# Modulation products in four PSUM strips of 32 partitions, added by a selector product, with the first stage reordered

## The chip, the cores and the metric

The kernel is one program on one core of a Trainium2 chip. The metric is device time in microseconds (us) of one execution. TensorE is called PE (its weight loads PEld), VectorE DVE, ScalarE ACT, GpSimd POOL; SP issues most transfers. A matmul below is written by its stationary operand (partitions*columns) and its moving operand (partitions x columns). A matmul of f32 operands is two records of the trace (two weight loads and two streams of the moving operand); one of fp32r operands is one record.

## What is computed

Two transformer blocks over 512 tokens of width 1024. What the change touches is the modulation of the first block: two vectors of 1024 (`c` and `c_ctx`) go through silu and a 1024 x 6144 matrix, and the results shift, scale and gate what follows.

```python
mod_x = (jax.nn.silu(c) @ w_ada[l] + b_ada[l])[:, None, :]
mod_c = jax.nn.silu(c_ctx) @ w_ada[l] + b_ada[l]
sh1, sc1, g1, sh2, sc2, g2 = jnp.split(mod_x, N_MOD, axis=-1)
csh1, csc1, cg1, csh2, csc2, cg2 = jnp.split(mod_c, N_MOD, axis=-1)

p_x = modulate(rmsnorm(h, norm_mix_w[l]), sh1, sc1) @ w_in[l]
p_c = modulate(rmsnorm(hc, norm_mix_w[l]), csh1, csc1) @ w_in[l]
# gated linear attention over x with the context's state, pooling, output matmul,
# gate g1; then 32 experts (top 4) with sh2, sc2, g2; then the second block
```

`h` has 512 rows (x), `hc` 256 rows (context).

## The kernel before

**The modulation matrix** is worked in 12 chunks of 512 columns. Chunks 0 and 1 are the first shift, 2 and 3 the first scale, and so on in pairs. A chunk is four pieces of 512 KB (each two blocks k of 128 rows), fetched by SP into a ring of 9 slots (`W`, `fetch`, L437); piece i is issued when the work on piece i-9 is done. The weights of the input projection (`in_w_in`) follow the first four chunks in the same ring.

**A chunk** (`ada_pe`, L839) is eight f32 matmuls whose stationary operand has 2 columns (`cc`, the silu of the two vectors, in the tile SM) and whose moving operand is 128x512 of the ring. All eight add into 2 partitions of one PSUM bank. Then ACT copies the 2x512 result (`ada_act`, L868; `ada_row`), PE turns it in four small transposes into 128 x 8 (`adat`), and DVE adds the bias into MOD (`ada_dve`, `add_ada`, L884).

**The first stage** (`mod_pe`, `mod_act`, `mod_dve`) has 8 sum-of-squares matmuls for x (moving 128x512) and 8 for the context (128x256) against a matrix of ones. ACT squares into two buffers, so that square k waits for matmul k-2. Then come chunks 0, 2, 1, 3 in that order. DVE makes variance and reciprocal root for x and for the context (ACT takes the root), normalises 8 blocks of each in turn, and then, for each half h, adds the modulation of chunks h and h+2 (`gm`), and shifts and scales four blocks of each (`ntmp`, `hn_low`) into pairs of fp32r parts. The projection (`proj_pe`) starts with the parts of half 0 and with the first split unit of `in_w_in` (`conv_lo`, L465).

**The later chunks.** Chunks 4 to 9 are `slow` jobs: generators that PE, ACT and DVE advance between the steps of the gated linear attention (`gla_pe`, L1533), half a chunk at a time. Those that are left when the attention ends run one after the other (`finish_all`). Chunks 10 and 11 follow at the start of `out_pe` (L1922), ahead of the output matmul; their four small matmuls come inside it. `gla_pe` also has matmuls on 64 rows of the array at a time: the updates of the state (64*128 with 64x256) go to rows 0 to 63 and 64 to 127 in turn (`hh`, L1574), with the two taking turns in the program's order.

The order on each engine is the order in which this code issues; nothing reorders it.

Of the kernel before, what the change touches and what calls it, by code (L numbers as in the profile page):

```python
# [334 lines left out]
def build(nc, ins, out):  # L335
# [3 lines left out]
    def sb(name, shape, dt=F32):  # L339
        return nc.alloc_sbuf_tensor(name, shape, dt)  # L340
# [3 lines left out]
    COLS = sb("COLS", [128, 160])  # L344
    MOD = sb("MOD", [128, 96])
    SM = sb("SM", [128, 256])
    BPT = sb("BPT", [128, 1536])

    base = (nc.sbuf_base + 31) // 32 * 32
# [30 lines left out]
    def pe(*key):  # L380
        return s_pe, at_pe[key]
# [36 lines left out]
    def bank_of(name):  # L418
        return PB[banks[name]] if name in banks else PB[0]
# [59 lines left out]
    def raw_tile(w):  # L479
        return place(w.base, w.kt * w.n).rearrange("p (a b) -> p a b", b=w.n)  # L480
# [303 lines left out]
    def load_dve(v):  # L784
        for k in range(8):
            v.wait_ge(*pe("xt", k))
            v.copy(hk(k), bank_of(("xt", k))[:, :])
            v.free(("xt", k))
        for k in range(8):
            v.wait_ge(*pe("ct", k))  # L790
            v.copy(HC[:, k, :], bank_of(("ct", k))[:, 0:256])
            v.free(("ct", k))
        v.wait_ge(*pe("cols"))
        v.copy(COLS[:, 0:n0 + 48], bank_of("cols")[:, 0:n0 + 48])
        v.free("cols")

    cc = SM[:, 0:16].rearrange("p (k s) -> p k s", s=2)
    HXh, HXl, HCh, HCl = r(10496, 4096, 512), r(14592, 4096, 512), r(18688, 2048, 256), r(20736, 2048, 256)  # L800
    sq1 = [a(8448, 512), a(8960, 512)]
    rx, rc = a(9472, 512), a(9984, 256)
# [9 lines left out]
    def sumsq_act(q, tag, src, nk, T, sq):  # L812
        for k in range(nk):
            if k >= 2:
                q.wait_ge(*pe("sumsq", tag, k - 2))
            q.act(sq[k % 2][:, 0:T], src(k), ACT.Square, ("square", tag, k))
# [22 lines left out]
    def ada_pe(p, c):  # L839

        key = ("ada", c)
        b = p.bank(key)
        p.inuse.append(b)
        w = None
        for k in range(8):
            if k % 2 == 0:
                w = W.raws[RAW_ADA[c] + k // 2]
                land(p, w)
            if k == 0:
                p.wait_ge(*act("silu c"))  # L850
                p.claim(key)
            p.mm(PB[b][0:2, :], cc[:, k, :], raw_tile(w)[:, k % 2, :], k == 0, k == 7, count=k % 2 == 1)
            if k % 2 == 1:
                p.note(w.done)
            if k == 3:
                yield
        p.note(("ada", c))
        p.inuse.remove(b)
        yield
        b = p.bank(("adat", c))  # L860
        p.wait_ge(*act("ada", c))
        p.claim(("adat", c))
        mr = ada_row(c)
        for j in range(4):
            p.tp(PB[b][:, 2 * j:2 * j + 2], mr[:, j * 128:(j + 1) * 128], ("adat", c) if j == 3 else None)
        yield

    def ada_act(q, c):  # L868
        yield
        q.wait_ge(*pe("ada", c))  # L870
        if c > 4:
            q.wait_ge(*pe("adat", c - 1))
        q.copy(ada_row(c), bank_of(("ada", c))[0:2, :], ("ada", c))
        q.free(("ada", c))
        yield
        yield
# [15 lines left out]
    RAW_ADA = [4 * FIRST.index(c) if c < 4 else 25 + 4 * (c - 4) for c in range(12)]  # L892

    def ada_row(c):
        return ar[0:2, c * 512:c * 512 + 512] if c < 4 else ar[0:2, 22272:22784]

    def mod_act(q):
        q.limit = U_IN
        q.wait_ge(*dve("all", "cols"))
        q.act(cc[:, :, 0], C("c", 0, 8), ACT.Silu)  # L900
        q.act(cc[:, :, 1], C("cctx", 0, 8), ACT.Silu, "silu c")
        sumsq_act(q, "x", hk, 8, 512, sq1)
        root2_act(q, "x", rx)
        sumsq_act(q, "ctx", lambda k: HC[:, k, :], 8, 256, sq1)
        root2_act(q, "ctx", rc)
        for h in range(2):
            for c in (h, h + 2):
                for _ in ada_act(q, c):
                    pass
            q.wait_ge(*dve("gm", h))  # L910
            for k in range(4 * h, 4 * h + 4):
                for s in range(2):
                    q.act((HXh, HCh)[s][:, k, :], normed_in(s, k), ACT.Identity, ("hn high", s, k), bias=M(0, k, s), scale=gm[:, k, s:s + 1])
            for u in (2 * h, 2 * h + 1):
                conv_hi(q, W, u)
# [3 lines left out]
        return XN[:, k, :] if s == 0 else HC[:, k, :]  # L919

    def mod_pe(p):
        sumsq_pe(p, "x", 8, 512, sq1)
        sumsq_pe(p, "ctx", 8, 256, sq1)
        turn = []
        for c in FIRST:
            part = ada_pe(p, c)
            next(part)
            next(part)
            for x in turn:
                for _ in x:  # L930
                    pass
            turn = [part]
        for _ in turn[0]:
            pass

    def mod_dve(v):
        v.limit = U_IN
        root1_dve(v, "x", 8, 512, rx, 1.0 / 1024)
        root3_dve(v, "x", rx)
        root1_dve(v, "ctx", 8, 256, rc, 1.0 / 1024)  # L940
        root3_dve(v, "ctx", rc)
        for k in range(8):
            v.stt(XN[:, k, :], hk(k), C("nmix", k), rx, ALU.mult, ALU.mult)
            v.stt(HC[:, k, :], HC[:, k, :], C("nmix", k), rc, ALU.mult, ALU.mult)
        for h in range(2):
            for c in (h, h + 2):
                for _ in ada_dve(v, c):
                    pass
            v.ts(gm[:, 4 * h:4 * h + 4, :], mcol[:, 8 + 4 * h:12 + 4 * h, :], 1.0, None, ALU.add, None, ("gm", h))
            ahead = None  # L950
            for k in range(4 * h, 4 * h + 4):
                for s in range(2):
                    v.ts(ntmp[s][k % 2], normed_in(s, k), gm[:, k, s:s + 1], M(0, k, s), ALU.mult, ALU.add)
                    if ahead:
                        hn_low(v, *ahead)
                    ahead = (s, k)
            hn_low(v, *ahead)
            for u in (2 * h, 2 * h + 1):
                conv_lo(v, W, u)
# [917 lines left out]
    def last_ada_act(q):  # L1877
        yield
        q.wait_ge(*pe("adat", 10))
        q.copy(ada_row(11), bank_of(("ada", 11))[0:2, :], ("ada", 11))  # L1880
        q.free(("ada", 11))
        yield
        for _ in range(2):
            yield
# [7 lines left out]
    def out_act(q):  # L1892
        q.limit = None
        for u in range(NUNIT):
            conv_hi(q, W, U_IN + u)
            split_act(q, "mix", mixp, lambda k: MX[:, k, :], range(2 * u, 2 * u + 2))
        q.wait_ge(*pe("ada", 10))
        q.copy(ada_row(10), bank_of(("ada", 10))[0:2, :], ("ada", 10))
        q.free(("ada", 10))
        q.slow += [last_ada_act(q), shift_act(q)]  # L1900
        tile = lambda c, m: q.jobs.append(tile_act(q, c * 4 + m))
        dense(q, conv_hi, W, [512], 8, tile)
        by_tiles(q, 1, tile)
        q.u += 4
# [2076 lines left out]
```

## Time and profile before

| | us |
|---|---|
| median of 3 runs | 3268.64 (3266.44 to 3270.3) |
| span of the profiled execution | 3265.2 |
| PE busy in it | 3061.1 (94%) |
| DVE busy | 2139.1 (66%) |
| ACT busy | 1639.6 (50%) |
| share of PE in the chain that ended last | 82% |
| HBM read | 608.10 MB |

Times of the trace are counted from the start of its span. The first stage lies before 76.7 us, the projection up to 198.6, the attention up to 355, the output matmul from 374.8; the experts and the second block, which the change doesn't touch, fill the rest. A record of a matmul includes some 0.16 us of its way through the array, so that ten records in a row take less than ten times the mean; the distance between starts is what a matmul costs in a row of them. In `windows`, PEclk is the granted clock as a share of 2.4 GHz.

### The profile page before, as it was taken

How to read it: one execution, taken by the hardware profiler on the slowest of the kernel's cores; microseconds unless marked ns; L12 is line 12 of the kernel's file. 1: busy time of each engine (PE TensorE's matmuls, PEld its weight loads, DVE VectorE, ACT ScalarE, POOL GpSimd, SP SyncE). 2: the span in 40 equal slices, each digit the busy share in tenths (PEclk: the TensorE clock that was granted, in tenths of full speed). 3: DMA queues.
4: the chain of work that ended last, by engine and by line, in shares of the span. 5: the costliest groups of instructions: out<-in, count | busy, mean ns of one | idle time of the engine just before them, and what ended most of it. 6: DMA issues, size and time to landing. Idle time of an engine off the chain costs nothing.

```text
span 3265.2 us, 36970 instructions
## 1 busy us (share of the span) xinstructions
PE 3061.1 (94%) x13794; PEld 2398.3 (73%) x13794; DVE 2139.1 (66%) x2425; ACT 1639.6 (50%) x1933; POOL 261.3 (8%) x234
## 2 busy tenths in 40 slices
PE   6989989999999999999979977999998987999998
PEld 2865467777777777777767756888886765888887
DVE  4555449999999999999966444443446557443445
ACT  3332338878887788778753213332235237332334
POOL 1053720000000000000010000000000000000000
PEclk9998969999999999999988978999999997999999
DMA  6244749999999999999963202323232220223210
GB/s 214 70 132 155 234 157 375 363 378 373 377 364 372 379 376 372 363 377 377 363 205 134 84 29 88 96 91 103 91 108 74 84 59 1 84 91 103 91 65 26
DMA packets 225085, 643.10 MB, mean 197 GB/s; under 512 B 20054, under 2 KB 38516, under 8 KB 224036
## 3 DMA queue, kind: packets, MB, share of 16 engines
q1 hardware_dynamic: 207984, 577.70, 48.8%
q0 software_dynamic: 12816, 51.39, 5.7%
q10 hardware_dynamic: 4100, 11.59, 0.9%
q8 instruction: 110, 1.80, 0.2%
q14 instruction: 75, 0.61, 0.1%
HBM read 608.10 MB, written 32.51 MB: 196 GB/s over the span
## 4 chain that ended last, share of the span: by engine, by line
PE 82%; DVE 11%; ACT 3%; issue 2%; DMA 1%; DVEq 0%; ACTq 0%; SPq 0%; POOLq 0%
PE ps L272 80%; PE ps L288 3%; DVE arena L192 2%; DVE arena L203 2%; DVE arena L199 2%; ACT wunits L463 1%; DVE ring_r L471 1%; ACT arena L237 1%; DVE arena_r L203 1%; DVE arena L215 1%; DVE arena L211 1%; DMA arena<-in_ctx 1%; DVE arena_r L471 1%; DVE H L192 0%; DMA sum_scratch<-arena 0%
## 5 line engine op out<-in xcount | busy, mean ns | idle before, releaser
L471 DVE TENSOR_TENSOR ring_r<-ring,wunits 128x1024 fp32r<-128x1024 f32 x795 | 949.5, 1219 | 659.8 <-ACT wunits L463 636.2
L463 ACT ACTIVATE wunits<-ring 128x1024 fp32r<-128x1024 f32 x795 | 834.6, 1054 | 809.3 <-PE ps L272 797.3
L272 PE MATMUL ps<-arena_r,wunits 128*128 128x512 f32 (+1 forms) x3552 | 1111.9, 395 | 15.5 <-DVE arena_r L192 6.9
L272 PE MATMUL ps<-wunits,arena_r 128*128 128x512 f32 x3520 | 991.3, 399 | 7.0 <-DVE arena_r L192 7.0
L272 PEld LDWEIGHTS ps<-arena_r,wunits 128*128 128x128 f32 x3552 | 671.5, 190 | 165.1 <-issue 16.6
L272 PEld LDWEIGHTS ps<-wunits,arena_r 128*128 128x128 f32 x3520 | 658.5, 189 | 152.4 <-DVE arena_r L192 8.9
L272 PE MATMUL ps<-arena_r,ring_r 128*128 128x512 f32 (+1 forms) x1776 | 695.1, 391 | 0.0
L272 PE MATMUL ps<-ring_r,arena_r 128*128 128x512 f32 x1280 | 410.3, 391 | 0.0
L272 PEld LDWEIGHTS ps<-arena_r,ring_r 128*128 128x128 f32 x1776 | 337.5, 190 | 70.5
L471 DVE TENSOR_TENSOR arena_r<-arena,wunits 128x1024 fp32r<-128x1024 f32 x240 | 284.9, 1221 | 16.6 <-ACT wunits L463 9.4
L463 ACT ACTIVATE wunits<-arena 128x1024 fp32r<-128x1024 f32 x240 | 254.3, 1061 | 65.6 <-PE ps L272 63.5
L272 PEld LDWEIGHTS ps<-ring_r,arena_r 128*128 128x128 f32 x1280 | 241.1, 188 | 53.2 <-issue 2.2
L272 PE MATMUL ps<-arena 128*128 128x128 f32 (+11 forms) x1074 | 194.0, 368 | 42.6 <-DVE arena L207 15.2
L237 ACT ACTIVATE arena<-ps 128x512 f32<-128x512 f32 (+6 forms) x190 | 121.4, 639 | 197.0 <-PE ps L272 143.6
L272 PEld LDWEIGHTS ps<-arena 64*128 64x128 f32 (+5 forms) x1074 | 135.7, 203 | 101.9 <-issue 42.7
L288 PE MATMUL ps<-KC,arena 128*128 128x128 f32 (+3 forms) x854 | 126.4, 290 | 73.7 <-DVE arena L203 37.9
L288 PEld LDWEIGHTS ps<-KC,arena 128*128 128x128 f32 (+3 forms) x854 | 102.1, 151 | 105.7 <-DVE arena L203 54.7
L272 PE MATMUL ps<-arena_r 128*128 128x512 f32 (+3 forms) x520 | 160.0, 392 | 0.9 <-DVE arena_r L197 0.9
L237 ACT ACTIVATE arena<-arena 128x512 f32<-128x512 f32 (+5 forms) x140 | 73.7, 527 | 135.5 <-DVE arena L192 84.0
L2360 POOL DMA_INDIRECT sum_scratch<-arena x33 | 52.4, 1587 | 1037.3 <-ACT arena L237 1037.3
L192 POOL TENSOR_TENSOR ring<-ring 128x512 f32<-128x512 f32 (+5 forms) x90 | 105.5, 1173 | 193.5 <-DVE ring L192 140.4
L192 DVE TENSOR_TENSOR arena<-ps,arena 128x512 f32<-128x512 f32 (+1 forms) x115 | 78.7, 684 | 61.7 <-PE ps L272 51.2
(171 smaller groups left out, 1928.5 us busy)
## 6 DMA issues: line engine op xcount, KB each, us to landing
ring<-in_w_gu SPq DMA_DIRECT2D x382, 512.0 KB, 8.5
ring<-in_w_down SPq DMA_DIRECT2D x170, 512.0 KB, 6.1
arena<-in_w_gu SPq DMA_DIRECT2D x146, 512.0 KB, 8.2
arena<-in_w_down SPq DMA_DIRECT2D x94, 512.0 KB, 6.4
ring<-in_w_ada SPq DMA_DIRECT2D x48, 512.0 KB, 4.7
ring<-in_ffn_w_gate SPq DMA_DIRECT2D x44, 512.0 KB, 3.5
ring<-in_ffn_w_up SPq DMA_DIRECT2D x44, 512.0 KB, 3.5
ring<-in_ffn_w_down SPq DMA_DIRECT2D x40, 512.0 KB, 3.6
```

Of the source, the lines that this page charges most:

```text
L192: self.inc(self.e.tensor_tensor(o, x, y, op), key)
L199: self.inc(self.e.tensor_scalar(o, x, s1, s2, op0, op1), key)
L203: self.inc(self.e.scalar_tensor_tensor(out=o, in0=x, scalar=s, in1=y, op0=op0, op1=op1), key)
L211: self.inc(self.e.reciprocal(o, x), key)
L215: self.inc(self.e.tensor_reduce(o, x, AX.X, op), key)
L237: self.inc(self.e.activation(o, x, f, **kw), key)
L272: ins = self.e.matmul(o, l_, r_, start=start, stop=stop, skip_group_check=True)
L288: ins = self.e.transpose(o, x, self.ident[0:k, 0:k])
L463: q.inc(q.e.activation(h, raw, ACT.Copy), (st.tag, "hi", i))
L471: q.inc(q.e.tensor_tensor(lo, raw, h.bitcast(F32), ALU.subtract), (st.tag, "lo", i))
L2360: g.e.indirect_dma_start(out=sum_d, out_offset=bass.IndirectOffsetOnAxis(ap=idx, axis=0), in_=YB[i], in_offset=None, compute_op=ALU.add).t ...
```

## The change

- The silu values move from SM to a tile of their own, CW (48 columns, filled with zeros once). The stationary operand of product k is now the 32 columns from 2k on: its first two are the silu values of block k, the rest are those of later blocks or zeros.
- Product k writes PSUM partitions 32(k mod 4) to 32(k mod 4)+31. Blocks k and k+4 add up in one strip, so a bank holds four partial sums, with the wanted rows at partitions 0, 1, 32, 33, 64, 65, 96 and 97.
- ACT copies 128x512 in the place of 2x512. The four transposes become four ordinary f32 matmuls: stationary 128*128 of the copied rows, moving the 128x2 selector `strips`, which has a one where the partition is 0 or 1 within its strip; they turn and add the strips at once. DVE makes `strips` in the load stage, with a fill and a reduction, ahead of its copy of COLS.
- The first stage is in another order: products of chunks 0 and 2, sum of squares of x, small matmuls of chunks 0 and 2, products of chunks 1 and 3, sum of squares of the context, small matmuls of chunks 1 and 3. ACT and DVE follow that order. DVE now normalises all of x ahead of the variance of the context.
- Order and number of the products in the later stages stay as they are.

```diff
+    CW = sb("CW", [128, 48])
...
+        v.fill(CW[:, :], 0.0)
+        v.wait_ge(*loaded("kc"))
+        v.reduce(strips, ident.rearrange("p (j c) -> p c j", c=32)[:, 0:2, :], ALU.add)
         v.wait_ge(*pe("cols"))
         v.copy(COLS[:, 0:n0 + 48], bank_of("cols")[:, 0:n0 + 48])
...
-            p.mm(PB[b][0:2, :], cc[:, k, :], raw_tile(w)[:, k % 2, :], k == 0, k == 7, count=k % 2 == 1)
+            strip = slice(32 * (k % 4), 32 * (k % 4) + 32)
+            p.mm(PB[b][strip, :], CW[:, 2 * k:2 * k + 32], raw_tile(w)[:, k % 2, :], k < 4, k >= 4,
+                 count=k % 2 == 1)
...
-            p.tp(PB[b][:, 2 * j:2 * j + 2], mr[:, j * 128:(j + 1) * 128], ("adat", c) if j == 3 else None)
+            p.mm(PB[b][:, 2 * j:2 * j + 2], mr[:, j * 128:(j + 1) * 128], strips, j == 0, j == 3,
+                 ("adat", c) if j == 3 else None)
...
-        q.copy(ada_row(c), bank_of(("ada", c))[0:2, :], ("ada", c))
+        q.copy(ada_row(c), bank_of(("ada", c))[:, :], ("ada", c))
...
         sumsq_act(q, "x", hk, 8, 512, sq1)
+        for c in (0, 2):
+            for _ in ada_act(q, c):
+                pass
         root2_act(q, "x", rx)
         sumsq_act(q, "ctx", lambda k: HC[:, k, :], 8, 256, sq1)
+        for c in (1, 3):
+            for _ in ada_act(q, c):
+                pass
         root2_act(q, "ctx", rc)
...
+        for cs, tag, T in (((0, 2), "x", 512), ((1, 3), "ctx", 256)):
+            products = [ada_pe(p, c) for c in cs]
+            for x in products:
+                next(x)
+                next(x)
+            sumsq_pe(p, tag, 8, T, sq1)
+            for x in products:
                 for _ in x:
                     pass
```

PE at the start of the first stage, before (-) and now (+). `ring,SM` and `ring,CW` are products of chunks, `arena,KC` the sums of squares, `KC,arena` 128x2 the transposes and `SM,arena` 128x2 the selector products; the first number of a shape is the number of partitions written.

```order
+L272 MATMUL ps<-ring,CW 32x512 x16
 L272 MATMUL ps<-arena,KC 128x512 x8
+L272 MATMUL ps<-SM,arena 128x2 x8
+L272 MATMUL ps<-ring,CW 32x512 x16
 L272 MATMUL ps<-arena,KC 128x256 x8
-L272 MATMUL ps<-ring,SM 2x512 x16
-L288 MATMUL ps<-KC,arena 128x2 x4
-L272 MATMUL ps<-ring,SM 2x512 x8
-L288 MATMUL ps<-KC,arena 128x2 x4
-L272 MATMUL ps<-ring,SM 2x512 x8
-L288 MATMUL ps<-KC,arena 128x2 x8
+L272 MATMUL ps<-SM,arena 128x2 x8
```

The 32 products of the first four chunks stand 16 ahead of the sum of squares of x and 16 ahead of that of the context, where all stood behind both.

DVE in the load stage and the first stage, before (-) and now (+); COLS holds the transposed vectors, L199 and L211 make the reciprocal root, L203 normalises, L895 adds the bias of a chunk.

```order
+L223 MEMSET CW 128x48
+L215 TENSOR_REDUCE SM<-KC 128x2
 L207 COPY COLS<-ps 128x158
 L199 TENSOR_SCALAR arena<-ps 128x512
 L211 RECIPROCAL arena<-arena 128x512
+L203 SCALAR_TENSOR_TENSOR arena<-H,COLS,arena 128x512 x8
+L895 TENSOR_TENSOR MOD<-ps,COLS 128x8 x2
 L199 TENSOR_SCALAR arena<-ps 128x256
 L211 RECIPROCAL arena<-arena 128x256
-L203 SCALAR_TENSOR_TENSOR arena<-H,COLS,arena 128x512
-L203 SCALAR_TENSOR_TENSOR arena<-arena,COLS 128x256
```

The eight blocks of x and two additions of chunks now stand ahead of the context's variance; before, x and the context took turns behind both roots (the last two rows eight times).

## Rows read from the trace of the kernel before

**Rows 1.** Timeline of PE, first stage: start, length (us), engine, line, operation, operands, count, [idle before].

```profile
28.01 9.41 PE L272 MATMUL ps<-arena,KC 128*128 128x512 f32 x16 [5.40 <-ACT arena L237]
...
44.15 13.90 PE L272 MATMUL ps<-ring,SM 128*2 128x512 f32 x32
57.98 0.41 PE L288 MATMUL ps<-KC,arena 2*128 2x2 f32 x4
...
76.70 1.22 PE L272 MATMUL ps<-arena_r,wunits 128*128 128x512 f32 x2 [0.98 <-DVE ring_r L471]
```

**Rows 2.** Timeline of DVE, first stage.

```profile
38.93 3.35 DVE L211 RECIPROCAL arena<-arena 128x512 f32<-128x512 f32 x1 [0.69 <-ACT arena L237]
44.26 0.42 DVE L199 TENSOR_SCALAR arena<-ps 128x256 f32<-128x256 f32 x1 [1.98 <-PE ps L272]
...
56.90 0.48 DVE L203 SCALAR_TENSOR_TENSOR arena<-arena,COLS 128x256 f32<-128x256 f32 x1
...
65.91 0.17 DVE L197 TENSOR_SCALAR SM<-MOD 128x8 f32<-128x8 f32 x1
```

**Rows 3.** Timeline of ACT, first stage.

```profile
26.76 0.45 ACT L237 ACTIVATE SM<-COLS 128x8 f32<-128x8 f32 x2
...
36.32 1.28 ACT L237 ACT_TABLE_LOAD   x1
```

**Rows 4.** DMA issues in 21.7 to 22.5 and in 46 to 47: count, KB, us to landing.

```profile
ring<-in_w_ada SPq DMA_DIRECT2D x2, 512.0 KB, 11.4
...
ring<-in_w_ada SPq DMA_DIRECT2D x1, 512.0 KB, 3.6
```

**Rows 5.** Windows: stretch, length, busy time (records) by engine, PEclk, DMA share, GB/s.

```profile
28.00:31.00 3.00, 2.99 (x4) 1.38 (x5) 0.00 (x0) 1.16 (x2) 0.00 (x0) 0.50 1.05 384
...
244.00:249.00 5.00, 5.00 (x24) 4.88 (x24) 3.48 (x7) 0.00 (x0) 0.00 (x0) 0.50 0.18 68
```

**Rows 6.** Timeline of PE, attention and start of the output matmul.

```profile
258.91 3.59 PE L272 MATMUL ps<-ring,SM 128*2 128x512 f32 x8
...
269.75 5.11 PE L272 MATMUL ps<-arena 64*128 64x64 f32 x32 [1.26 <-DVE arena L203]
274.79 5.13 PE L272 MATMUL ps<-ring,SM 128*2 128x512 f32 x8
...
304.38 1.23 PE L272 MATMUL ps<-arena 64*128 64x256 f32 x4 [4.64 <-DVE BPT L192]
...
325.13 1.13 PE L272 MATMUL ps<-arena 64*128 64x256 f32 x8
...
334.30 3.39 PE L272 MATMUL ps<-arena 64*128 64x64 f32 x32
...
339.87 7.03 PE L272 MATMUL ps<-ring,SM 128*2 128x512 f32 x16
347.57 0.40 PE L288 MATMUL ps<-KC,arena 2*128 2x2 f32 x4 [0.68 <-ACT arena L237]
...
355.95 10.46 PE L272 MATMUL ps<-ring,SM 128*2 128x512 f32 x24
369.59 5.29 PE L272 MATMUL ps<-ring,SM 128*2 128x512 f32 x8 [3.18 <-DMA ring<-in_w_ada]
...
403.28 0.95 PE L272 MATMUL ps<-KC,arena 128*128 128x2 f32 x8
```

**Rows 7.** Timeline of DVE, attention and start of the output matmul.

```profile
268.19 1.51 DVE L203 SCALAR_TENSOR_TENSOR arena<-arena,ps 128x256 f32<-128x256 f32 x3 [2.52 <-PE ps L272]
...
287.09 1.56 DVE L1678 COPY_PREDICATED arena<-arena,ps 128x512 f32<-128x512 uint32 x2 [3.92 <-PE ps L272]
...
359.23 1.22 DVE L471 TENSOR_TENSOR ring_r<-ring,wunits 128x1024 fp32r<-128x1024 f32 x1
```

**Rows 8.** Chain that ended last, in order of time: start, us, what.

```profile
359.57 9.97 DMA ring<-in_w_ada
```

**Rows 9.** Timeline of the weight loads of PE at the start of the products.

```profile
44.15 0.09 PEld L272 LDWEIGHTS ps<-ring,SM 128*2 128x2 f32 x2 [0.33 <-issue]
```

More of the change, by code:

```diff
@@ L795, in load_dve @@
         v.free("cols")
-    cc = SM[:, 0:16].rearrange("p (k s) -> p k s", s=2)
+    cc = CW[:, 0:16].rearrange("p (k s) -> p k s", s=2)
+    strips = SM[:, 16:18]
     HXh, HXl, HCh, HCl = r(10496, 4096, 512), r(14592, 4096, 512), r(18688, 2048, 256), r(20736, 2048, 256)
@@ L894, in ada_row @@
     def ada_row(c):
-        return ar[0:2, c * 512:c * 512 + 512] if c < 4 else ar[0:2, 22272:22784]
+        return a(c * 512, 512) if c < 4 else a(22272, 512)
     def mod_act(q):
@@ L902, in mod_act @@
         sumsq_act(q, "x", hk, 8, 512, sq1)
+        for c in (0, 2):
+            for _ in ada_act(q, c):
+                pass
         root2_act(q, "x", rx)
         sumsq_act(q, "ctx", lambda k: HC[:, k, :], 8, 256, sq1)
+        for c in (1, 3):
+            for _ in ada_act(q, c):
+                pass
         root2_act(q, "ctx", rc)
         for h in range(2):
-            for c in (h, h + 2):
-                for _ in ada_act(q, c):
-                    pass
             q.wait_ge(*dve("gm", h))
@@ L921, in mod_pe @@
     def mod_pe(p):
[L922 to L929, printed above, removed]
+        for cs, tag, T in (((0, 2), "x", 512), ((1, 3), "ctx", 256)):
[5 more added lines that the diff above has]
+            for x in products:
                 for _ in x:
                     pass
-            turn = [part]
-        for _ in turn[0]:
-            pass
     def mod_dve(v):
@@ L939, in mod_dve @@
         root3_dve(v, "x", rx)
+        for k in range(8):
+            v.stt(XN[:, k, :], hk(k), C("nmix", k), rx, ALU.mult, ALU.mult)
+        for c in (0, 2):
+            for _ in ada_dve(v, c):
+                pass
         root1_dve(v, "ctx", 8, 256, rc, 1.0 / 1024)
@@ L942, in mod_dve @@
         for k in range(8):
-            v.stt(XN[:, k, :], hk(k), C("nmix", k), rx, ALU.mult, ALU.mult)
             v.stt(HC[:, k, :], HC[:, k, :], C("nmix", k), rc, ALU.mult, ALU.mult)
+        for c in (1, 3):
+            for _ in ada_dve(v, c):
+                pass
         for h in range(2):
-            for c in (h, h + 2):
-                for _ in ada_dve(v, c):
-                    pass
             v.ts(gm[:, 4 * h:4 * h + 4, :], mcol[:, 8 + 4 * h:12 + 4 * h, :], 1.0, None, ALU.add, None, ("gm", h))
@@ L1879, in last_ada_act @@
         q.wait_ge(*pe("adat", 10))
-        q.copy(ada_row(11), bank_of(("ada", 11))[0:2, :], ("ada", 11))
+        q.copy(ada_row(11), bank_of(("ada", 11))[:, :], ("ada", 11))
         q.free(("ada", 11))
@@ L1897, in out_act @@
         q.wait_ge(*pe("ada", 10))
-        q.copy(ada_row(10), bank_of(("ada", 10))[0:2, :], ("ada", 10))
+        q.copy(ada_row(10), bank_of(("ada", 10))[:, :], ("ada", 10))
         q.free(("ada", 10))
```

## The prediction

> **What bounds the kernel now.** I read the PE timeline of the first 77 us first. The sums of squares come first and end at 37.4; 32 products (64 records) begin at 44.15, and 16 of them take 13.90 us [rows 1]. So a product costs 0.87 us and a chunk 6.9, though only 2 columns of the array are used. DVE is done with both normalisations at 57.4 and gets the scale of half 0 only at 65.91 [rows 2]: 8.5 us in which it waits for products of chunk 2. From there it needs 10.8 us of shifting, scaling and splitting until the projection starts at 76.70 [rows 1]. The bound up to 66 is therefore PE's products, and behind them a DVE sequence that is nearly as late.
>
> Then I read PE and DVE side by side in the attention. DVE waits for PE at 268.19 and 287.09 [rows 7], with products ahead of both; at 304.38 it is the other way, PE has been idle for 4.64 us [rows 6], so products there cost nothing. Chunks 8, 9 and 10 and 11 run with nothing beside them from 339.87 on, with ACT's copy in the path of each (idle 0.68), and end at 374.9 after a wait on a piece of the matrix [rows 6, 8].
>
> **Do strips overlap?** Everything hangs on this, and no row of before has column strips. The nearest rows are row strips: eight records of 64*128 with 64x256 that take turns between rows 0 to 63 and 64 to 127 take 1.13 us at 325.13 [rows 6]. One record of 512 columns costs 0.43 in a row of them [rows 1], so one of 256 costs 0.215; eight in a row with the 0.16 at the end would be 1.9, and four times two at once 1.02. The two strips do overlap, and both records of an f32 matmul do. I take the same for four column strips: two groups of four products, each 2 x 0.43, so a chunk of 1.72 us plus the end. Bounds: 1.7 (full) and 6.9 (none); half overlap gives 3.5.
>
> The weight loads of the products run under the stream before them: the first two are both at 44.15 [rows 9], while the first stream has only begun, and the streams stay 0.43 apart [rows 1]. The Trainium skill (TensorE: Matmul & The Clock Gate, Part 3) says that loads overlap with running matmuls only where the row group differs, which would speak against column strips; these loads are of the same row group and overlap, so the trace disagrees. The same section says that matmuls start strictly in program order; since both records of a product go to one strip, that rule would leave two strips at once, which is rival B below. It also lists 3.07 times for four row strips and 2.38 for three column strips, from which an estimate for a chunk is 2.2 us; the four chunks that are in a row on the path would then be some 2 us slower in all than in my sum.
>
> **First stage.** Silu is ready at 27.2 [rows 3], where PE was idle. The products of chunks 0 and 2 go there. The ring's DMA is full at 384 GB/s in 28 to 31, 1.37 us a piece [rows 5]; of the nine first pieces the last two are issued about 21 and 22 and take 11.4 [rows 4], so piece 7 lands near 32 and PE ends at 33 whatever the overlap gives. The clock is at 0.50 (1.2 GHz) in that stretch either way [rows 5]. Eight sums at 0.86 bring x to 40.0, against 37.4. The fill and the reduction on DVE ahead of COLS (0.17 each, as its smallest operations) delay silu by 0.35, which is hidden behind the pieces; without that cover they would cost it.
>
> Then DVE: variance and root 2.1 (0.6 more than before, since ACT has two copies and the 1.28 table load [rows 3] in front), reciprocal 3.35, eight blocks of x at 0.78, two additions 0.4, context variance to reciprocal 2.7 (44.26 to where the first normalisation could start, 46.95, as the 16 blocks end at 57.4) [rows 2], eight blocks of 0.52, two additions and the scale 0.6. That is 19.7 after 40.0, so half 0 starts at 59.7 against 66.1: **6.4 us**. Is PE in time? Selector products to 42; pieces 8 to 15 are released from 29 on and land, one in 1.37 us behind piece 8 at 33, by 42.6; products of chunks 1 and 3 end at 45.6 (under them the same 3.6 us from issue to landing as in rows 4), context sums at 50, DVE asks at 52.2. A margin of 2 us. PE is then idle until 70 and begins the projection at the low clock for longer than before (two records took 1.22 there already): 0.5 lost. Net **5.9**.
>
> **Attention.** Half a chunk falls from 3.43 to 0.86. Chunk 4: 5.1 less on PE ahead of 268.19, of which DVE's own work behind its 2.52 us wait lets through **4.4**. Chunk 5: first half 5.13 [rows 6], slower than the 3.59 of chunk 4 since the clock was low at its start, saves 3.4, second half 2.6, ahead of 287.09 with its 3.92 wait: **6.0**. Chunk 6: **0**, hidden by the 4.64 of slack. Chunk 7: 4.4 by the same pattern as chunk 4, less 0.5 for its selector products on the path: **3.9**.
>
> **Selector products.** Eight records with stationary 128*128 and moving 128x2 take 0.95 at 403.28 [rows 6], against 0.41 for the four records of the transposes [rows 1]: 0.54 a chunk. ACT's copy works on the 128 partitions side by side, so I cost it as before. In chunks 4 to 6 this lies in idle time. For 10 and 11 it stands in the dense output matmul: **1.1 lost**.
>
> **Chunks 8 to 11.** From 339.87 to 374.9 it is 35.0 us. Chunk 8 is now 1.9, copy 0.68, selector 0.95, chunk 9 the same: 7.1, chunk 10 to 8.9. Now DMA is next. The pieces of chunk 11 wait for slots of chunk 9's last piece (5.4) and of chunk 10's first three (7.5 to 8.9); with 3.6 from issue to landing and 1.37 each behind the output weights in the same queue they land at 13.5, 15, 16.2 and 17.6, so the products end at 18.5. The wait of 9.97 [rows 8] was long because a large POOL transfer shared the DMA; it now comes later than these. DVE is nearly as late: its first split unit of the output weights was at 359.23 [rows 7], 19.4 into the stretch, behind its wait for chunks 8 and 9; without that wait it is at 15.4, and the parts of the first block at 17.4. So 18.6 against 35.0: **16.3**.
>
> **The clock** takes some back. A stretch of small matmuls is at 0.50 although PE is busy all the time (244 to 249), and 32 records of 64x64 took 5.11 at 269.75 and 3.39 at 334.30 [rows 5, 6]. The long streams of the products stood between such groups; with a quarter of their length the transposes, norms and 64-column groups behind chunks 5, 7 and 11 may stay at 1.2 GHz. Bounds 0 and 10, the latter if all those are as slow as at 269.75; I take **6 lost**.
>
> **Sum:** 5.9 + 4.4 + 6.0 + 3.9 + 16.3 - 1.1 - 6 = 29.4. The profiled span of 3265.2 becomes 3235.8. The median of the runs stands 3.4 above the span, so 3239 us. What follows (projection, experts, second block) is unchanged and moves as a whole.
>
> **Rivals.**
> A. Full overlap, as summed: 3239, with 3232 (no clock loss, some of the DMA wait smaller) to 3249 (clock loss of 10 and the stretch of chunks 8 to 11 bounded 6 later). Chance 0.70.
> B. Strips overlap by halves, because the two records of a product bind its strip and starts are in program order: chunk 3.5. First stage: x at 43.1, products of 1 and 3 end at 52, context sums at 56.5, so gain 1.8. Chunks 4, 5 and 7: 3.4 + 4 + 3. Chunks 8 to 11: 10.2 for two, DMA end at 20, gain 15. Less 1.1 and 3: 23, so 3246. For it speaks the page's rule; against it the 1.13 us. Chance 0.14.
> C. No overlap: each product streams alone, 0.87 as now. Then the new order hurts: x sums end at 27.5 + 2 + 13.9 + 6.9 = 50.3, selectors 52.2, products of 1 and 3 to 66.1, context sums to 70, and 7.9 of DVE behind: half 0 at 77.9, 11.3 later than now. Selector products add 0.54 each for chunks 7 to 11, 2.7. 3268.6 + 14 = 3283. It turns from gain to loss where a chunk takes more than about 5 us. For it: no row of before has four streams of full height from the same partitions at once. Chance 0.12.
> D. Strips overlap but something else holds the attention and the start of the output matmul (POOL's long sequence, the router's weights), so that only the first stage and part of the rest come through: 3262. Chance 0.04.
>
> **Numbers.** Likeliest 3239. The range takes in A and B with their bounds, 3227 to 3256; C and D are left out. Differences under 0.2% (6.5 us) can't be told from no change here. Faster 0.84 (A and B), same 0.04 (D), slower 0.12 (C).
>
> **What would show it.** Four product records starting within hundredths, a chunk of about 1.9 us, in PE's timeline; x sums ending at 40 and DVE's scale of half 0 at 59.5; projection at 70.3; chunks 8 to 11 in under 20 us with the last wait on the matrix's pieces; PEclk under before's between 270 and 340. Wrong if a chunk still takes 7 us, if the context sums end after DVE asks for them, or if the output matmul starts no earlier because POOL or DVE end last.

## The result

| | us |
|---|---|
| before, median of 4 runs | 3269.47 (3266.44 to 3274.62) |
| changed, median of 4 runs | 3240.76 (3238.89 to 3242.27) |
| ratio | 0.9913, 95% interval 0.9899 to 0.9927 |
| span of the profiled execution | 3240.1 (before 3265.2) |
| predicted | 3239 (3227 to 3256) |

The kernel is faster by 28.7 us in the medians and by 25.1 in the two spans; the profiled execution of the changed kernel was the slowest of its four. The forecast of full overlap held. That the median lies within 2 us of the forecast is in part luck: the terms add up to 29.4 us against 25.1 in the two traces (the span was to be 3235.8 and is 3240.1), and the forecast then put the median 3.4 above the span, where it is 0.7 above it. The two largest terms were too high.

### The profile after

PE's timeline of the first stage, which answers to [rows 1]: start, length, engine, line, operation, operands, count, idle before.

```profile
29.05 6.07 PE L272 MATMUL ps<-ring,CW 128*32 128x512 f32 x32 [5.29 <-ACT CW L237]
35.05 7.52 PE L272 MATMUL ps<-arena,KC 128*128 128x512 f32 x16
42.41 1.84 PE L272 MATMUL ps<-SM,arena 128*128 128x2 f32 x16
44.18 3.64 PE L272 MATMUL ps<-ring,CW 128*32 128x512 f32 x32
...
73.18 1.22 PE L272 MATMUL ps<-arena_r,wunits 128*128 128x512 f32 x2 [18.73 <-DVE ring_r L472]
```

The 32 records of chunks 1 and 3 take 3.64 us, where 32 records took 13.90. Half a chunk (x8) takes 1.06 to 1.07 us against 3.59. Four records start together and the next four 0.43 us later: full overlap. At 1.2 GHz, as for chunks 0 and 2, it is 0.85 (starts at 29.054, 29.061, 29.068 and 29.074, the next four from 29.879 and then from 30.732). The Trainium skill (TensorE: Matmul & The Clock Gate, Part 3) gives 2.38 times for three column strips and 3.07 for four row strips; this trace shows 3.4 times for half a chunk and 3.8 for the row of two chunks. Rival B, which its rule on the order of starts would have given, did not come.

DVE in the first stage, which answers to [rows 2]:

```profile
62.39 0.17 DVE L197 TENSOR_SCALAR SM<-MOD 128x8 f32<-128x8 f32 x1
62.59 1.00 DVE L199 TENSOR_SCALAR arena<-arena,SM,MOD 128x512 f32<-128x512 f32 x2
```

DVE no longer waits for products here (before, it waited 7.12 us for the transposes of chunk 2, up to 65.71). PE waits for DVE, 18.73 us in a row.

PE in the attention and at the start of the output matmul, which answers to [rows 6]:

```profile
263.98 4.43 PE L272 MATMUL ps<-arena 64*128 64x64 f32 x32 [1.43 <-DVE arena L203]
...
294.84 1.22 PE L272 MATMUL ps<-arena 64*128 64x256 f32 x4 [6.41 <-DVE BPT L192]
...
319.48 3.39 PE L272 MATMUL ps<-arena 64*128 64x64 f32 x32 [0.73 <-DVE arena L203]
...
323.71 1.66 PE L272 MATMUL ps<-arena,KC 128*128 128x512 f32 x2
325.17 1.91 PE L272 MATMUL ps<-BPT,KC 128*128 128x512 f32 x2
327.01 2.16 PE L272 MATMUL ps<-ring,CW 128*32 128x512 f32 x16
...
337.38 3.30 PE L272 MATMUL ps<-ring,CW 128*32 128x512 f32 x16 [2.75 <-DVE BPT L192]
342.60 1.05 PE L272 MATMUL ps<-ring,CW 128*32 128x512 f32 x4 [1.92 <-DMA ring<-in_w_ada]
...
349.98 0.70 PE L272 MATMUL ps<-arena_r,wunits 128*128 128x512 f32 x2 [2.33 <-DVE arena_r L192]
...
351.50 1.05 PE L272 MATMUL ps<-arena_r,wunits 128*128 128x512 f32 x2
```

Set beside the same places before (269.75, 304.38, 334.30, 339.87, 374.81), these starts are 5.8, 9.5, 14.8, 12.9 and 24.8 us earlier. From chunk 8 to the output matmul it is 22.97 us, where it was 34.94 and 18.6 was forecast. PE waits for three things there: for a PSUM bank (2.75), for pieces of chunk 11 (1.92, then some 0.3 for each of the other three), and for DVE (2.33). Before, it waited for one piece (3.18) and for neither of the others.

The chain that ended last, in that place, shows the last one from DVE's side:

```profile
339.88 1.95 DVE SM L197
...
342.05 1.84 DVE SM L207
...
344.15 1.70 issue
345.86 1.22 DVE ring_r L472
...
347.17 2.67 DVE arena_r L192
```

Operations on 128x8 elements take 1.95 and 1.84 us. Their like before the change took 0.17 to 0.2 each, save one of 2.24.

Where the gain between chunk 4 and the output matmul comes from, by groups of PE's rows in 257 to 375 before and in 255.8 to 350 now (busy us, mean ns; idle before). Before:

```profile
L272 PE MATMUL ps<-ring,SM 128*2 128x512 f32 x128 | 60.1, 620 | 3.2 <-DMA ring<-in_w_ada 3.2
L288 PE MATMUL ps<-KC,arena 2*128 2x2 f32 x24 | 2.6, 209 | 1.4 <-ACT arena L237 1.4
```

Now:

```profile
L272 PE MATMUL ps<-ring,CW 128*32 128x512 f32 x128 | 21.0, 685 | 5.5 <-DMA ring<-in_w_ada 2.8 <-DVE BPT L192 2.8
L272 PE MATMUL ps<-SM,arena 128*128 128x2 f32 x48 | 7.1, 270 | 1.5 <-ACT arena L237 1.5
L272 PE MATMUL ps<-arena 64*128 64x256 f32 x66 | 11.6, 424 | 9.7 <-DVE BPT L192 6.4 <-DVE arena L192 2.5 <-DVE arena L203 0.8
```

From the start of chunk 4 to that of the output matmul it was 115.9 us and is 92.6, which is 23.3 less. Products give 39.1 us. Of these 4.5 go to the selector products, 1.6 to all other matmuls (45.3 to 46.9 in sum, counted between these two starts), and 9.6 to new idle time of PE (11.6 to 21.2).

### The profile page after: what moved, and what is told of

The parts are those of the page before. It is cut to its first block, busy times and chain, and to the rows that moved or that the text cites. A ratio compares the mean times of both kernels' runs of the same rounds, so it can differ in the third digit from the quotient of the medians.

```text
span 3240.1 us, 37063 instructions
## 1 busy us (share of the span) xinstructions
PE 3012.4 (93%) x13842; PEld 2398.4 (74%) x13842; DVE 2147.3 (66%) x2427; ACT 1639.8 (51%) x1933; POOL 261.0 (8%) x234
## 4 chain that ended last, share of the span: by engine, by line
PE 81%; DVE 13%; ACT 3%; issue 2%; DMA 1%; DVEq 0%; ACTq 0%; SPq 0%; POOLq 0%
PE ps L272 78%; PE ps L288 3%; DVE arena L203 2%; DVE arena L192 2%; DVE ring_r L472 2%; DVE arena L199 2%; ACT wunits L464 1%; ACT arena L237 1%; DVE arena L211 1%; DVE arena_r L203 1%; DMA arena<-in_ctx 1%; DVE arena L215 1%; DVE H L192 0%; DVE arena_r L192 0%; DMA sum_scratch<-arena 0%
## 5 line engine op out<-in xcount | busy, mean ns | idle before, releaser
L472 DVE TENSOR_TENSOR arena_r<-arena,wunits 128x1024 fp32r<-128x1024 f32 x240 | 285.2, 1222 | 16.4 <-ACT wunits L464 8.3
L237 ACT ACTIVATE arena<-ps 128x512 f32<-128x512 f32 (+5 forms) x190 | 121.5, 639 | 158.5 <-PE ps L272 107.8
L288 PE MATMUL ps<-KC,arena 128*128 128x128 f32 (+2 forms) x806 | 122.0, 296 | 71.4 <-DVE arena L203 39.3
L288 PEld LDWEIGHTS ps<-KC,arena 128*128 128x128 f32 (+2 forms) x806 | 98.8, 152 | 97.9 <-DVE arena L203 56.0
```

Of the source, the lines that this page charges most:

```text
L237: self.inc(self.e.activation(o, x, f, **kw), key)
L288: ins = self.e.transpose(o, x, self.ident[0:k, 0:k])
L472: q.inc(q.e.tensor_tensor(lo, raw, h.bitcast(F32), ALU.subtract), (st.tag, "lo", i))
```

## The experiments

The theory: strips run side by side and are the whole cause; behind them DVE sets the end of the first stage, and DVE, the pieces and POOL the start of the output matmul. All times are medians, with the lowest and the highest; the kernel before, run beside each group, was at 3267.6 to 3268.8.

### The strips without the reorder

```diff
-        for cs, tag, T in (((0, 2), "x", 512), ((1, 3), "ctx", 256)):
...
+        sumsq_pe(p, "x", 8, 512, sq1)
+        sumsq_pe(p, "ctx", 8, 256, sq1)
+        turn = []
+        for c in FIRST:
```

(and `mod_act` and `mod_dve` as before)

> The strips alone: four strips and the selector products as in the changed kernel, but the first stage in the order of the kernel before (both sums of squares, then chunks 0, 2, 1, 3; DVE normalises x and the context in turn). Theory 1, the reorder costs: the products of chunks 0 and 2, worked at the low clock, push the sums of x back from 37.4 to 42.6, and everything on DVE follows; with strips and the old order the products of chunks 0 and 2 are done by about 52, well before DVE has normalised its 16 blocks (57.4 before, some 1 us later with the later load stage), so the scale of half 0 comes at 58.5 to 60 in the place of 62.4, and the time is 3236 to 3239, 2 to 5 us under the changed kernel (3240.8). Theory 2, the reorder is needed, since the first chunks have to lie in the gap where silu is ready and the squares are not: the scale of half 0 comes at 64 or later and the time is 3243 or more. The attention and the output matmul should be as in the changed kernel under both.

3239.8 us (3237.9 to 3246.4), ratio 0.9915 (0.9901 to 0.9929): the same as the changed kernel. The 2 to 5 us did not come, and neither did theory 2. PE, then DVE:

```profile
47.47 3.64 PE L272 MATMUL ps<-ring,CW 128*32 128x512 f32 x32
...
70.41 3.57 PE L272 MATMUL ps<-SM,arena 128*128 128x2 f32 x16 [8.40 <-ACT arena L237]
73.84 1.20 PE L272 MATMUL ps<-arena_r,wunits 128*128 128x512 f32 x2
```

```profile
47.57 0.42 DVE L199 TENSOR_SCALAR arena<-ps 128x256 f32<-128x256 f32 x1 [3.00 <-PE ps L272]
...
61.68 0.17 DVE L197 TENSOR_SCALAR SM<-MOD 128x8 f32<-128x8 f32 x1
```

The x sums end at 39.7, 2.9 earlier, but DVE then waits 3.00 for the context's sums, and half 0 begins at 61.89, only 0.7 earlier. That is given back on PE: the selector products of chunks 1 and 3, whose copies on ACT come behind half 0, stand in front of the projection and run at the low clock (3.57). So with strips the reorder is worth nothing that these runs can tell (3239.8 against 3240.8).

### The reorder without the strips

> The reorder alone: products with 2 stationary columns into one place of 2 partitions, transposes as before, first stage in the new order. Theory 1 (products do not overlap without strips, rival C of the prediction without its selector products): 32 records of 0.87 us apart stand ahead of the sums of x, which end near 50; half 0 at about 78 against 66.1; time 3280 (3277 to 3284), 11 to 12 us slower than before. Theory 2, that the reorder itself brings part of the gain of the first stage: 3268 or less.

3280.3 us (3279.1 to 3283.9), ratio 1.0036 (1.0022 to 1.0049), as theory 1 says.

```profile
27.13 16.23 PE L272 MATMUL ps<-ring,SM 128*2 128x512 f32 x32 [4.74 <-ACT SM L237]
43.29 7.52 PE L272 MATMUL ps<-arena,KC 128*128 128x512 f32 x16
```

The x sums end at 50.8 and the scale of half 0 is made at 77.50 (forecast in rival C: 50.3 and 77.9). The reorder alone costs 11.5 us (3280.3 against 3268.8).

### One strip, two strips

```diff
-            strip = slice(32 * (k % 4), 32 * (k % 4) + 32)
-            p.mm(PB[b][strip, :], CW[:, 2 * k:2 * k + 32], raw_tile(w)[:, k % 2, :], k < 4, k >= 4,
+            strip = slice(32 * (k % 1), 32 * (k % 1) + 32)
+            p.mm(PB[b][strip, :], CW[:, 2 * k:2 * k + 32], raw_tile(w)[:, k % 2, :], k < 1, k >= 7,
```

(two strips: `k % 2`, `k < 2`, `k >= 6`; copies and selector of 32 or 64 partitions)

> The changed kernel with one strip: all eight products of a chunk write PSUM partitions 0 to 31 with the same 32 stationary columns, ACT copies 32 partitions, the selector products contract 32; new order, same number of instructions. Only the place of the products differs from the changed kernel. Theory 1, the gain is the overlap of strips: starts stay 0.43 apart (0.87 a product), a chunk takes 7 us, and with the selector products the time is 3283 (3280 to 3287). Theory 2, the gain comes from elsewhere (32 columns in the place of 2, the selector form): near 3241.

> The changed kernel with two strips (block k to strip k mod 2), 64 partitions copied and contracted; new order. Theory 1, the time of a chunk goes as one over the number of strips: chunk of 3.5 to 3.7 us at the high clock (four strips 2.0, one 7.0), half chunk 1.9; first stage 0 to 2 us better than before, chunks 4, 5 and 7 about 3 each, chunks 8 to 11 about 13, less selector products: 3250 (3246 to 3254). Theory 2, two strips already give all that four do (two streams at most at once): chunk near 2 us and time near 3241.

One strip: 3281.3 us (3280.6 to 3286.1), ratio 1.0037 (1.0024 to 1.0050). Two strips: 3247.2 us (3243.7 to 3248.4), ratio 0.9934 (0.9918 to 0.9949). Half a chunk and a whole one at the high clock, one strip first, then two:

```profile
274.70 3.62 PE L272 MATMUL ps<-ring,CW 128*32 128x512 f32 x8
...
369.50 7.05 PE L272 MATMUL ps<-ring,CW 128*32 128x512 f32 x16
```

```profile
259.23 1.91 PE L272 MATMUL ps<-ring,CW 128*32 128x512 f32 x8
...
337.53 3.63 PE L272 MATMUL ps<-ring,CW 128*32 128x512 f32 x16
```

3.62, 1.91 and 1.06 for one, two and four strips: 3.4 us over their number, plus a tail of about 0.2. Only the place of the products differs between these kernels, and it decides 40 us. The kernel's time does not follow as one over the number: two strips bring 34 of the 40 us.

### The last four chunks in one strip

```diff
+            n = 4 if c < 8 else 1
-            strip = slice(32 * (k % 4), 32 * (k % 4) + 32)
+            strip = slice(32 * (k % n), 32 * (k % n) + 32)
```

> The changed kernel, but chunks 8 to 11 use one strip (32 partitions copied and contracted), chunks 0 to 7 four. Theory: this stretch took 34.9 us before and 23.0 now; with one strip it is back to 35 and 1 more for the selector products of 8 and 9, so 12 to 14 us of the 28 come from it: time 3254 (3252 to 3256). Rival: DVE and POOL are the bound at the start of the output matmul and the products of these chunks are half hidden: 3246 to 3250.

3252.5 us (3249.1 to 3255.9), 11.8 over the changed kernel. In its trace chunk 8 starts at 324.09 and the output matmul at 360.12: 36.0 us, 13.0 more than in the changed kernel. So this stretch is worth 12 to 13 us.

### What holds the output matmul

In these two, POOL leaves out the last of the six doublings of its table of powers and fills that half with zeros, so that the table is incomplete. In the second it also sends the table only behind chunk 11.

```diff
-        while m_ < 64:
+        g.fill(WR_[:, :, 32:64], 0.0)
+        g.fill(WI_[:, :, 32:64], 0.0)
...
+        while m_ < 32:
...
+        g.wait_ge(*pe("ada", 11))
         g.own()
         g.e.dma_start(ww_d, BUF).then_inc(s_wwd, 16)
```

> The changed kernel, but POOL leaves out the last doubling of its table of powers (6 operations of 128x1024 of the 24 in a row) and fills that half with zeros, so that its output isn't the reference's. Theory: the start of the output matmul (349.98 in the changed kernel, after 2.33 us of waiting for DVE) is held by DVE, whose small operations from 337 on run at 1.8 to 2.0 us in the place of 0.17 because POOL works until 349; with POOL done by about 338 they return to 0.17, the first parts are there at 345, and chunk 11 (ends 347.65, paced by its pieces) is the bound: output matmul at 347.7, time 3238.5 (3236 to 3240). Rival 1: DVE's operations are slow for another reason; they stay at 1.8 to 2.0 and the start stays at 350. Rival 2: the shorter POOL also lets transfers start earlier and delays the pieces of chunk 11: start at 350 or later with the wait on DMA.

> The run with the shorter POOL sequence (last doubling of the powers left out, that half filled with zeros, so the output isn't the reference's), and POOL sends its table to memory only once PE is done with chunk 11. There the DVE operations had returned to 0.17 us, but the table's transfer, sent at 335.6, delayed the pieces of chunk 11 (6.42 us of waiting for them) and the output matmul started at 351.3. Theory (two gates behind the products: DVE slowed by POOL, then the pieces slowed by POOL's transfer): with both away chunk 11 is paced by its pieces alone and ends about 10 us after chunk 10 starts, the output matmul starts 20 to 21 us after the start of chunk 8 (23.0 in the changed kernel, 26.0 with the shorter POOL alone): time 3238 (3236 to 3240). Rival (the pieces are late for another reason, such as the wait of chunk 10 for its bank): 23 us or more, 3241 or more.

Shorter POOL: 3242.7 us (3240.1 to 3244.1). DVE and then PE in its trace:

```profile
337.32 0.17 DVE L197 TENSOR_SCALAR SM<-MOD 128x8 f32<-128x8 f32 x1
...
338.14 0.17 DVE L192 TENSOR_TENSOR SM<-MOD,SM 128x8 f32<-128x8 f32 x1
```

```profile
346.25 5.12 PE L272 MATMUL ps<-ring,CW 128*32 128x512 f32 x16 [6.42 <-DMA ring<-in_w_ada]
351.30 0.73 PE L272 MATMUL ps<-arena_r,wunits 128*128 128x512 f32 x2
```

DVE's small operations return from 1.94 to 0.17: POOL was their cause. But POOL then sends its 2048 KB at 335.6, while the first of chunk 11's pieces is under way and ahead of the other three, and PE waits 6.42 for the first: chunk 11 starts 20.9 us behind chunk 8, where it was 15.6. The stretch is 26.0 us, longer than the 23.0 of the changed kernel. The theory's half on DVE and rival 2 both came true.

With the transfer held back too: 3238.4 us (3237.3 to 3239.4).

```profile
325.05 2.04 PE L272 MATMUL ps<-ring,CW 128*32 128x512 f32 x16
...
341.48 1.05 PE L272 MATMUL ps<-ring,CW 128*32 128x512 f32 x4 [2.13 <-DMA ring<-in_w_ada]
342.83 3.85 PE L272 MATMUL ps<-ring,CW 128*32 128x512 f32 x12 [0.30 <-DMA ring<-in_w_ada]
...
346.61 0.73 PE L272 MATMUL ps<-arena_r,wunits 128*128 128x512 f32 x2
```

21.6 us, and the output matmul starts straight behind chunk 11. The forecast was 20 to 21. What is left of the gap to 18.6 is the pieces: chunk 11 starts 16.4 us behind chunk 8, where the first of its pieces was forecast at 13.5, and goes on at 1.35 us a piece. The wait for a bank, 3.37 us here, comes ahead of chunk 10, and the next run shows that it is not what holds chunk 11.

### Another bank

```diff
-        b = p.bank(key)
+        b = p.bank(key, [p.banks["o", 1, hl] for hl in range(2)] if c >= 10 else ())
```

> The changed kernel, with chunks 10 and 11 kept out of the two PSUM banks that DVE's head norm still reads. In the changed kernel chunk 10 waits 2.75 us for such a bank (337.38). Theory: that wait is not on the path. Chunk 10 starts some 2.7 us earlier against the end of chunk 9, chunk 11 ends up to 2.7 earlier, and PE then waits the longer for DVE's first parts, so the output matmul starts at the same distance (23.0, at least 22.5) from the start of chunk 8: time 3241 (3239 to 3243), no difference. Rival: the bank is the gate, since through it the pieces of chunk 11 are issued later: output matmul 2.3 to 2.7 us earlier, 3238.

3238.0 us (3236.0 to 3241.2). The time is 2.8 under the changed kernel, below the range of the theory and at the rival's value, but the two were timed on different occasions, and the medians alone can't decide it. The trace does:

```profile
326.36 2.16 PE L272 MATMUL ps<-ring,CW 128*32 128x512 f32 x16
...
333.91 2.05 PE L272 MATMUL ps<-ring,CW 128*32 128x512 f32 x16
342.17 5.63 PE L272 MATMUL ps<-ring,CW 128*32 128x512 f32 x16 [6.21 <-DMA ring<-in_w_ada]
349.33 0.70 PE L272 MATMUL ps<-arena_r,wunits 128*128 128x512 f32 x2 [1.53 <-DVE arena_r L192]
```

Chunk 10 starts 2.8 us nearer to chunk 8 (7.6 us behind its start, against 10.4 in the changed kernel), and the output matmul stands where it stood, 22.97 behind chunk 8. The wait for the bank was not on the path. It would not be with DVE in time either: chunk 11 starts 15.8 us behind chunk 8 without that wait and 15.6 with it, since it is its pieces that arrive then; PE only waits for them in the place of the bank (6.21). With the early squares (below) it is 16.5 without and 16.3 with.

### Better orders of the first stage

First: sums of x, products of 0 and 2, sums of the context, selector products, products of 1 and 3.

```diff
+        sumsq_pe(p, "x", 8, 512, sq1)
+        for cs in ((0, 2), (1, 3)):
+            products = [ada_pe(p, c) for c in cs]
...
+            if cs[0] == 0:
+                sumsq_pe(p, "ctx", 8, 256, sq1)
```

> Another order of the first stage with the strips: sums of squares of x first, then the products of chunks 0 and 2, then the sums of the context, then the selector products of 0 and 2, products of 1 and 3, selector products of 1 and 3; ACT takes the root of x ahead of the squares of the context; DVE adds chunks 0 and 2 between variance and reciprocal of the context. Theory (DVE is the chain from the end of the x sums to half 0): x sums end at 39.7 as in the kernel with the strips alone, DVE has normalised x at 51, the context at 57.8, and half 0 begins at 58.5 to 60 against 62.6 in the changed kernel, projection at 69.5 to 71 against 73.2; time 3237 (3235 to 3240). Rival (the pieces of chunks 1 and 3 or PE come last): the additions of chunks 1 and 3 are waited for, half 0 at 62 or later, time 3240 or more.

Second: ACT squares x in the load stage, PE sums it behind its transposes, and silu comes after.

```diff
-        all_wait(p, "cols")
+        p.note(("all", "cols"))
+        sumsq_pe(p, "x", 8, 512, sq1)
+        barrier_of(p, "cols")
...
-        all_wait(q, "cols")
+        q.note(("all", "cols"))
+        for k in range(8):
+            q.wait_ge(*dve("hk", k))
+            if k >= 2:
+                q.wait_ge(*pe("sumsq", "x", k - 2))
+            q.act(sq1[k % 2][:, 0:512], hk(k), ACT.Square, ("square", "x", k))
+        barrier_of(q, "cols")
```

> The order of the run before it (sums of x, products 0 and 2, sums of the context, products 1 and 3), and ACT squares the blocks of x in the load stage, as soon as DVE has copied each, while silu comes after; PE sums them right behind its transposes, from 23.8 on. Same theory: every us by which the x sums end earlier comes out at the projection. Sums of x 23.8 to 30.7 (at the low clock, 0.86 each), x normalised at 43, context sums by 42.5, context normalised at 50, half 0 at 50.5 to 52, projection at 61.5 to 63 against 73.2: time 3230 (3228 to 3233). Rival 1: the pieces of chunks 1 and 3, released by the products from 32 on, land by 46 or later and PE's products of them end after 50: half 0 at 54 to 56, time 3233 to 3236. Rival 2: what is won ahead of the projection is given back in the attention, where POOL's sequence or a transfer holds: 3237 or more.

The first: 3233.7 us (3231.0 to 3235.0), ratio 0.9895 (0.9879 to 0.9912), better than its range. The second: 3228.0 us (3227.0 to 3228.6), ratio 0.9878 (0.9862 to 0.9895), the lower end of its range; 12.7 us under the changed kernel. Counted from the kernel before, timed beside each, it is 39.5 us where the changed kernel has 28.7. PE of the first, then of the second:

```profile
28.92 9.21 PE L272 MATMUL ps<-arena,KC 128*128 128x512 f32 x16 [5.84 <-ACT arena L237]
...
67.74 1.22 PE L272 MATMUL ps<-arena_r,wunits 128*128 128x512 f32 x2 [12.13 <-DVE ring_r L472]
```

```profile
24.13 7.67 PE L272 MATMUL ps<-arena,KC 128*128 128x512 f32 x16
...
62.58 1.22 PE L272 MATMUL ps<-arena_r,wunits 128*128 128x512 f32 x2 [11.49 <-DVE ring_r L472]
```

From the end of the x sums to the projection it is 30.6 us in the changed kernel, 29.6 in the first and 30.8 in the second, where ACT loads two tables in a row (1.28 each): DVE's chain, whatever stands in front. The second is 5.2 ahead of the first at the projection and 2.2 at the output matmul (339.43 against 341.60). Some 1.5 of the lost 3 us go where its granted clock falls to 0.83 in both windows between 150 and 160; in the other kernel with early squares (below) it stays at 1.00 there, and that one is 4.0 ahead at its output matmul (337.64). What takes the rest stays open. At the end the two spans are 4.9 apart (3231.3 and 3226.4) and the medians 5.7, so the lead is not lost for good.

### The second of these with the other bank

> The run with the early squares of x, and the other banks for chunks 10 and 11 of the run before this one. By the theory that DVE's first parts hold the output matmul (it waits 1.22 us for them there), nothing or up to 0.3 us: 3228 (3226 to 3229). By the rival (bank is the gate): 3225.5.

3227.9 us (3225.0 to 3230.4): no difference, with the output matmul 22.62 behind chunk 8 (22.97 without). Its median and that of the run with early squares alone can't be told apart.

## Why the prediction was right, and where it was not

| term | predicted | in the two traces |
|---|---|---|
| first stage, to the projection | +6.4 | +3.5 (76.70 to 73.18) |
| low clock at its start | -0.5 | -0.9 (+2.6 left at 148.61) |
| from there to chunk 4 | 0 | -1.1 |
| chunk 4 | +4.4 | +4.2 |
| chunk 5 | +6.0 | +5.1 |
| chunk 6 | 0 | -1.3 |
| chunk 7, to 334.30 | +4.4 | +5.3 |
| from there to chunk 8 | -0.5 | -2.0 |
| chunks 8 to 11 | +16.3 | +12.0 |
| selector products of 10 and 11, and all that follows | -1.1 | +0.3 |
| clock | -6 | in the rows above, see below |
| sum | +29.4 | +25.1 |

The +0.3 is a net. At 357.97 the lead of 24.8 us is down to 22.8: the first matmuls of the output matmul run at the low clock (1.4 us, the record at 351.50), and the selector products of chunk 10 take 0.5. In the experts and the second block, which no edit touches, the distance between the two traces moves between 20.0 and 24.4 us before it ends at 25.1. The forecast that what follows moves as a whole holds for the end and not on the way; why is open.

**Overlap** was right: a chunk takes 1.9 us, the starts lie within hundredths, and the row strips of [rows 6] were the right nearest row. The runs with one, two and four strips show it as the cause.

**The first stage** was mis-sized at the start of DVE's chain, not in it. From the end of the x sums to half 0 it is 20.0 us (predicted 19.7). The x sums ended at 42.6 instead of 40.0. In that execution the transposes of the context started 1.15 us later than before, which no edit explains; in the 13 traces of this study they start between 20.1 and 21.5. The run with the shorter POOL, whose first stage is the same, has them at 20.34, and there the x sums end at 41.1 and the projection starts at 71.68: a gain of 5.0 where the forecast was 6.4. So of the 2.9 us that this term lacks, 1.5 belong to that execution and 1.4 to the forecast. The step that failed is "PE ends at 33 whatever the overlap gives": I took the last piece as the bound and silu's delay as hidden behind it. What bound was PE at the low clock: eight groups of four records from 29.05 on, the first seven 0.78 to 0.85 us apart, so the products ended at 35.1 (27.77 to 33.6 in the run with the shorter POOL). At 1.2 GHz sixteen products in front of the x sums are not free even with full overlap. I also never costed the strips in the old order; that run shows the reorder to be worth nothing, and the two after it that the sums belong first.

**The context sums** ended at 52.6, ahead of DVE's question at 55.0: the margin was 2.4 (predicted 2).

**Chunk 6** was hidden, as said. But DVE lost 1.6 us on two operations that ran beside POOL:

```profile
278.10 3.32 DVE L192 TENSOR_TENSOR arena<-arena 128x768 f32<-128x768 f32 x2
```

Before they took 1.68, since POOL's sequence had ended by then (287.71); now DVE is 11 us earlier and POOL is not.

**Chunks 8 to 11** is the term that failed by size, 12.0 for 16.3. The failing step is "without that wait it is at 15.4, and the parts of the first block at 17.4": I moved DVE's rows earlier at their old lengths. They came to lie beside POOL's long operations, which end at 349.3; in the kernel before these ended at 358.7, just ahead of DVE's first split at 359.23. The second step that was off is "they land at 13.5, 15, 16.2 and 17.6": the first piece let chunk 11 start at 15.6, and its products end at 20.6, not 18.5. Of the 4.4 us between 18.6 and 22.97, 2.1 are thus the pieces and 2.3 DVE behind them. The runs bear this out: 23.0 us in the changed kernel, 26.0 with a shorter POOL, whose transfer runs beside the pieces, and 21.6 with that transfer held back too, where DVE is in time and the pieces alone are left. The wait for a bank was not foreseen either, and cost nothing.

**The clock** was the right idea with a number too large for the matmuls I named. From chunk 4 to the output matmul, all matmuls but products and selector products took 1.6 us longer in sum; the sums of the second head norm (323.71 and 325.17) lost 1.4, and some others got shorter. With the 1.4 at the start of the output matmul that is 3.0 of the 6. The selector products took 0.8 over six times 1.05, and chunk 10 took 1.1 over the 2.16 of chunk 8: about 5 in all. The start of the projection lost another 0.9, where the forecast had 0.5. The first half of chunk 5 took 0.9 over its second; the forecast had left it 1.7, and it took 1.93. Another 1.7 us went in the projection, where nothing was changed:

```profile
160.00:165.00 5.00, 5.00 (x16) 3.06 (x15) 3.17 (x4) 4.53 (x4) 4.76 (x4) 0.87 0.35 108
165.00:170.00 5.00, 5.00 (x19) 3.98 (x18) 0.82 (x2) 3.55 (x3) 4.62 (x5) 0.79 0.00 0
```

The granted clock (third from the end) falls to 0.87 and 0.79 with PE busy all the time. It fell so in the runs with the shorter POOL, with POOL's store late and with another bank, but stayed at 1.00 in the one with the last four chunks in one strip, whose instructions are the same up to there, and in the kernel before. So no edit decides it by itself; what sets it off is not shown.

**Rivals.** C is what the kernel would have been without overlap (3283; measured 3281 with one strip); its 77.9 is 11.8 us behind the 66.1 of before, not 11.3. B matches the kernel with two strips (3246; 3247). D did not come as such, but its mechanism, POOL and DVE at the output matmul, is where 2.3 of the missing 4.3 us of the stretch of chunks 8 to 11 are.

## What to carry to other kernels

A matmul with at most 32 stationary columns and a long moving operand leaves room for three others beside it: put its blocks in strips of 32 PSUM partitions and add the strips with a selector in the transpose that follows anyway (0.95 to 1.05 us a chunk at 2.4 GHz, where the transposes took 0.41). When a stretch of PE shrinks, the waits behind it must be costed at the lengths that the engines have in their new company: here DVE met POOL, and a POOL transfer met the pieces. A wait in a trace is not yet a price: the one for a bank, 2.75 us, only stood in for a later one. What stands at the head of a long chain on one engine (the x sums) should stand first, and work that is made cheap need not be moved into a gap to hide it.

## What the runs showed of the hardware

- Column strips of f32 matmuls, two records each, run fully side by side: half a chunk 3.62, 1.91 and 1.06 us with one, two and four strips, 0.43 us a group of records at 2.4 GHz and 0.85 at 1.2.
- DVE and POOL exclude each other on some operations. A DVE operation on 128x8 elements in SBUF took 1.94 us beside POOL's operations on 128x1024 and 0.17 without them; one that reads PSUM (the addition at 339.67) took 0.17 beside them. Not every operation in SBUF was held: the one at 341.85, right behind one that was, took 0.17.

```profile
339.67 0.17 DVE L895 TENSOR_TENSOR MOD<-ps,COLS 128x8 f32<-128x8 f32 x1
339.88 1.94 DVE L197 TENSOR_SCALAR SM<-MOD 128x8 f32<-128x8 f32 x1
```

The Trainium skill (SBUF — State Buffer, SBUF: two separate sides) says that the two share a pair of ports under an exclusive lock, held for a whole instruction; the trace agrees, in that 1.94 and 1.81 us are within one POOL operation (2.29 us on average).
- The same 2048 KB transfer of POOL takes 6.6 us to land in the changed kernel and 10.3 where it overlaps with the pieces, the first of which then lets chunk 11 start 5.3 us later (20.9 behind chunk 8, for 15.6).
- The granted clock can drop in a dense stretch (0.87 and 0.79 in two windows of 5 us) and cost 1.7 us, and stay at 1.00 in a kernel with the same instructions up to there.
